# Two chained transformer blocks on one core: scaling the first block's attention queries whole, and moving its modulation sums to the end of a head

## The chip, the cores and the metric

One NeuronCore of a Trainium2 chip runs the whole program in one launch. The metric is the device time of that launch in microseconds (us), as the median of several runs. PE is TensorE (matrix products), DVE is VectorE, ACT is ScalarE, POOL is GpSimd and SP is SyncE, which here only issues transfers.

## The reference, cut to what matters

A first block (modulated normalisation, two kinds of attention, a gated feed-forward with a convolution) is followed by two layers of a second block. Everything is float32, 512 positions of 1024 features. The change lies in the first block's attention of eight heads, each with 64 unrotated and 32 rotated features:

```
mod = silu(c) @ w_ada + b_ada                # 6 * 1024 modulation values
sh1, sc1, g1, sh2, sc2, g2 = split(mod, 6)
h = rms_norm(x, g_mix_norm) * (1 + sc1) + sh1
q_lat, kv_lat, k_pe, qd, kd, vd = split(h @ w_in, SPLITS)
q = (rms_norm(q_lat, g) @ w_q_b).reshape(B, S, 8, 64 + 32)
q_nope, q_pe = rms_norm(q[..., :64], g), rope(rms_norm(q[..., 64:], g), positions)
kv = (rms_norm(kv_lat, g) @ w_kv_b).reshape(B, S, 8, 64 + 64)
k_nope, v = rms_norm(kv[..., :64], g), kv[..., 64:]
k_pe = rope(rms_norm(k_pe, g), positions)    # one rotated key part, shared by the 8 heads
o_mla = attention(cat(q_nope, q_pe), cat(k_nope, k_pe), v)
o_dil = dilated_attention(rope(norm(qd)), rope(norm(kd)), vd)
x = x + g1 * (cat(o_mla, o_dil) @ w_o)       # and then the feed-forward
```

## The kernel before

Each engine has a program of its own, written out by hand, and runs it strictly in that order. Semaphores tie the programs together: `at("head", t)` is the moment at which step `head` of tile `t` is done, and `wait_ge(*at(...))` waits for it.

**Weights** come as units of 1 MB, in the fixed order `STREAM`, through two buffers, `raw0` and `raw1`, in turn. SP issues unit v only when unit v-2, which lay in the same buffer, has been used. ACT copies a unit to a rounded high part (`split`, tile `whi`), DVE makes the low part (`wlo`), and PE does three products for each block (high x high, high x low, low x high; `mm3`).

Between the weight units lie units of `w_ada` for the modulation values. These aren't split. DVE's `ada_acc(a)` multiplies the eight parts of unit a by silu(c) and adds them up: two instructions on `128x256`, six more, and one that adds two halves. The raw buffer is free after the last of the six. PE's `ada_sums(a)` adds over the partitions, and DVE's `ada_out(a)` reads that sum into `mod`. The stream around the first block's heads is

```
a11, z8, a12, a13, z10, a14, a15, z12, a16, a17, z14, a18, a19, z16, wo0, wo1
```

where z8 to z16 are the units of the projections for the dilated attention and wo0 the first of `w_o`. So z10 comes into the buffer that a12 frees, z12 into that of a14, z14 into that of a16, z16 into that of a18, and wo0 into that of a19.

**Scaling.** After the projections, DVE works out the reciprocal roots r of all the norms. PE's `scale(t, b)` spreads the row of r that belongs to tile t over the partitions in PSUM bank b, and DVE's `head(t, b)` multiplies tile t by it: `qn` (unrotated query parts, 4 tiles of two heads), `qp` (rotated query parts, 2 tiles of four heads at 32 partitions each), `kn` (unrotated key parts), and `values_ok` for the values `vt`. The results of `qn` and `qp` go to `qt`, of `kn` to `kt`, where a head has 96 partitions. POOL sends the shared rotated key part to `kt` by a transfer once the last `qp` is scaled.

**The loop over heads.** In head h, PE does half of a projection tile (`z_half(h+2, 0)`), transposes two of the three parts of the probabilities (`head_turn(h, (0, 1))`), does the other half, transposes the last part (`head_turn(h, (2,))`), and then does the scores of head h+1, a row of statistics, the products with the values (`head_mix`), and `ada_sums(11 + h)`. ACT does, in this order, the split of the next z unit if h is odd (`split(9 + h // 2)`), the copies out of the transposes (`head_turned(h)`), the copies of the projection tile (`z_out`), and the exponentials of head h+1. The last part of `head_turn` waits for the first copy of `head_turned`. DVE finds the row maxima of head h+1 (`head_top`), multiplies a rotated tile by sines (`sine`) and does the sums `ada_acc`. POOL does the rest of the rotation (`rotate`) on `z` tiles.

Of the kernel before, what the change touches and what calls it, by code (L numbers as in the profile page):

```python
# [13 lines left out]
P = 128  # L14
S = 512
# [45 lines left out]
UNITS = split_units()  # L61
# [132 lines left out]
def build(nc, wstream, ada_in, x_in, pos_in, cols_in, layer_in, const_in, strip_in, bucket_in, rel_in, lru_in, y_out):  # L194
    scratch = nc.dram_tensor("bias_by_distance", (8, 640), F32, kind="Internal").ap()
    strips_dram = nc.dram_tensor("bias_strips", (8, P, S), F32, kind="Internal").ap()
    with ExitStack() as ctx:
# [51 lines left out]
        qn, qp, kn = region("qn", 17, [P, 4, S]), region("qp", 21, [P, 2, S]), region("kn", 4, [P, 4, S])  # L249
        qt, kt_ = region("qt", 9, [P, 8, S]), region("kt", 17, [P, 8, S])  # L250
        mla_out = [(region(f"mla_hi{i}", 9 + 2 * i, [P, S], F32R), region(f"mla_lo{i}", 10 + 2 * i, [P, S], F32R)) for i in range(4)]
        vt, zv = region("vt", 25, [P, 4, S]), region("zv", 17, [P, 4, S])
# [156 lines left out]
        def pe_program(pe):  # L409
# [231 lines left out]
            def head_scores(h, *free):  # L641
                for step in free:
                    pe.wait_ge(*at(*step))
                pe.wait_ge(*at("head", ("kn", h // 2)))
                pe.wait_ge(*at("k_pe"))
                if h > 0:
# [19 lines left out]

            def head_values(h):

                pe.wait_ge(*(at("values_ok", h // 2) if h < 8 else at("tile", ("z", 8 + (h - 8) // 2))))
                if h:  # L670
                    pe.wait_ge(*at("turned", h - 1, 1))
                src = vt[:, h // 2, :] if h < 8 else zv[:, (h - 8) // 2, :]
                for j in range(4):
                    ins = pe.transpose(ps[:, 4, P * j:P * (j + 1)], src[:, P * j:P * (j + 1)], C("ident"))
                ins.then_inc(*inc("values", "values", h))

            def head_turn(h, banks):
                maps = E[h % 2] if h < 8 else E_pair[h // 2][h % 2]
                pe.wait_ge(*(at("exp", h) if h < 8 else at("norm", h)))
                for b in banks:  # L680
                    if b == 2:
                        pe.wait_ge(*at("turned", h, 0))
                    elif b == 1 and h % 2 == 0:
                        pe.wait_ge(*at("vtok", h))
                    else:
                        pe.wait_ge(*(at("turned", h - 1, 2 - b) if h else at("head", ("kn", 2))))
                    for j in range(4):
# [57 lines left out]
            for n, t in enumerate(PROJECTED):  # L745
# [13 lines left out]
                if t == ("v", 2):  # L759
                    scale(("qn", 1), 0, ("head", "pe"))  # L760
                    scale(("qn", 2), 1, ("head", ("qn", 0)))
            z_half(0, 0, 6, ("sin", ("qp", 1)))
            scale(("qn", 3), 0, ("head", ("qn", 1)))
            scale(("qp", 0), 1, ("head", ("qn", 2)))
            z_half(0, 1, 6)
            scale(("qp", 1), 0, ("head", ("qn", 3)))
            statistics(("z", 0))
            scale("rms", 1, ("head", ("qp", 0)))
            scale(("kn", 0), 3)
            z_half(1, 0, 6, ("moved", ("z", 0)))  # L770
            scale(("kn", 1), 5, ("tile", ("v", 2)))
            z_half(1, 1, 6)
            scale(("kn", 2), 3, ("head", ("kn", 0)))
            scale(("kn", 3), 5, ("head", ("kn", 1)))
            head_scores(0, ("values_ok", 3), ("head", ("qp", 1)))
            statistics(("z", 1))
            head_values(0)
            for h in range(8):
                z_half(h + 2, 0, 6, ("moved", ("z", h + 1)) if h < 7 else ("tile", ("z", 8)))
                if h % 2 == 0 and h:  # L780
# [9 lines left out]
                if h < 7:  # L790
                    head_scores(h + 1)
                if h == 0:
                    head_turn(h, (2,))
                if h < 6:
# [5 lines left out]
                head_mix(h, *([("head", ("kn", 3))] if h == 0 else []))  # L800
                ada_sums(11 + h, 3, 0)
# [328 lines left out]
        def act_program(act):  # L1130
# [212 lines left out]
            for t in PROJECTED:  # L1343
# [8 lines left out]
                if t == ("kn", 1):  # L1352
                    split(7)
            head_seed("kv", 2, 10, KV_EPS)
            z_out(0, 6)
            split(8)
            z_out(1, 6)

# [41 lines left out]
            for h in range(8):  # L1400
                if h % 2 == 0 and h:
                    pair_out(h // 2 - 1)
                if h % 2:
                    split(9 + h // 2)
                if h == 0:
                    z_out(h + 2, 6)
                head_turned(h)
                if h:
                    z_out(h + 2, 6)
                if h == 5:  # L1410
# [240 lines left out]
        def dve_program(dve):  # L1651
# [284 lines left out]
            def head(t, b):  # L1936
# [10 lines left out]
                elif t[0] == "qp":  # L1947
                    dve.wait_ge(*at("roped", t))
                    for i in range(4):
                        w = slice(32 * i, 32 * i + 32)  # L1950
                        ins = dve.tensor_tensor(qt[64:96, 4 * t[1] + i, :], tile[w], ps[w, b, :], ALU.mult)
                else:
                    dve.wait_ge(*at("roped", t))
                    ins = dve.tensor_tensor(tile, tile, bank(b, rows), ALU.mult)
# [24 lines left out]
            head(("qn", 2), 1)  # L1979
            head(("qn", 3), 0)  # L1980
            head(("qp", 0), 1)
            head(("qp", 1), 0)
            sine(("z", 0))
            dve.wait_ge(*at("scale", "rms"))
            for i in range(4):
                dve.wait_ge(*at("tile", ("v", i)))
                dve.tensor_tensor(vt[:, i, :], vt[:, i, :], bank(1), ALU.mult).then_inc(*inc("values_ok", "values_ok", i))
            head(("kn", 0), 3)
            split(8)
            head(("kn", 1), 5)  # L1990
            head(("kn", 2), 3)
            head(("kn", 3), 5)


            def head_top(h):
                dve.wait_ge(*at("scores", h))
                if h == 0:
                    dve.wait_ge(*at("strip", 0))
                if h >= 2:
                    dve.wait_ge(*at("turn", h - 2, 2))  # L2000
# [62 lines left out]

            head_top(0)
            sine(("z", 1))
            ada_acc(11)
            for h in range(8):
                if h:
                    ada_out(10 + h, 3, 0)
                if h % 2 == 0 and h:  # L2070
                    pair_out(h // 2 - 1)
                if h == 6:
                    head_root("z", 7, 16, EPS[0:16])
                ada_acc(12 + h)
                if h % 2:
# [8 lines left out]
                if h % 2:  # L2084
                    pair_otok(h // 2)
            ada_out(18, 3, 0)
            pair_top(4, 0)
            pair_out(3)
            head(("z", 1), 7)
# [465 lines left out]
        def sp_program(sp):  # L2555
# [20 lines left out]
            for v in range(1, len(STREAM)):  # L2576
                load(v)
            for j, n in ((0, 2), (2, 2), (4, 2), (6, 1), (7, 1)):
                sp.wait_ge(*at("y", j + n - 1))
# [188 lines left out]
```

## Time and profile before

| | |
|---|---|
| Median of 3 runs | 2580.55 us (2578.91 to 2582.14) |
| Profiled execution, its own time | 2578.19 us |
| Its span | 2576.9 us |
| PE busy | 2530.8 us, 98% of the span |
| DVE, ACT, POOL busy | 1243.1, 953.3, 173.8 us |
| PE busy from 100 to 150 us | 40.85 of 50 us |
| PE busy from 500 to 1000 us | 500.00 of 500 us |

The span goes from the first to the last instruction. The first block's heads lie from about 150 to 253 us. In the rows below, a row of the timeline gives start, duration, engine, line, operation, output and inputs, and the count of merged instructions. A bracket at its end is the idle time of that engine just before it, and who ended it.

### The profile page before, as it was taken

To read this page: it belongs to the slowest core of one execution; us is meant where nothing else is said; L and a number is where in the kernel's file an instruction comes from. 1 tells how busy PE (TensorE), PEld (TensorE's weight loads), DVE (VectorE), ACT (ScalarE), POOL (GpSimd) and SP (SyncE) were. 2 spreads that over 40 slices of the span, in tenths; PEclk is the share of its full clock that TensorE was granted. 3 is DMA by queue.
4 is the path that set the end of the run, shared out by engine and by line. 5 is a ranking of instruction groups with operands and counts; after the bars stand their busy time and mean duration, and the time that the engine had idled before them with its cause. 6 is when DMAs were issued, how large, how long until landed. Compare 5 with 4: busy or idle time off the path is not lost.

```text
span 2576.9 us, 27632 instructions
## 1 busy us (share of the span) xinstructions
PE 2530.8 (98%) x11505; PEld 2052.2 (80%) x11505; DVE 1243.1 (48%) x1773; ACT 953.3 (37%) x1296; POOL 173.8 (7%) x172
## 2 busy tenths in 40 slices
PE   8989999999999999999999999999999999999998
PEld 5668778888888888878788888888888777888886
DVE  6677666654343333355743333433333466533333
ACT  5456544443232222335532222322222355422221
POOL 1121000000001110000011100011100000011100
PEclk9999999999999999999999999999999999999999
DMA  7333123333322222322232223222222322222231
GB/s 291 140 107 135 50 81 106 126 113 100 113 98 98 98 98 98 121 93 66 82 102 96 97 98 115 98 98 98 99 98 98 123 73 83 93 93 94 96 115 65
DMA packets 41390, 267.20 MB, mean 104 GB/s; under 512 B 5449, under 2 KB 5833, under 8 KB 11698
## 3 DMA queue, kind: packets, MB, share of 16 engines
q1 hardware_dynamic: 37440, 256.92, 29.1%
q0 software_dynamic: 2576, 7.10, 0.8%
q8 instruction: 91, 1.49, 0.2%
q10 hardware_dynamic: 1250, 1.42, 0.2%
q14 instruction: 33, 0.27, 0.0%
HBM read 262.78 MB, written 4.21 MB: 104 GB/s over the span
## 4 chain that ended last, share of the span: by engine, by line
PE 95%; DVE 3%; issue 1%; ACT 1%; DMA 0%; SPq 0%; DVEq 0%; ACTq 0%
PE ps L412 29%; PE ps L414 29%; PE ps L413 29%; PE ps L965 1%; PE ps L691 1%; PE ps L708 1%; PE ps L650 1%; PE ps L999 1%; DVE wlo L1655 0%; PE ps L580 0%; PE ps L664 0%; PE ps L986 0%; DMA early<-ada_in 0%; PE ps L582 0%; PE ps L581 0%
## 5 line engine op out<-in xcount | busy, mean ns | idle before, releaser
L1655 DVE TENSOR_TENSOR wlo<-raw,whi 128x2048 fp32r<-128x2048 f32 x213 | 488.1, 2292 | 1066.6 <-ACT whi L1137 1066.5
L412 PE MATMUL ps<-ahi,whi 128*128 128x512 f32 x2272 | 895.9, 394 | 1.3 <-ACT tmp L1321 1.3
L414 PE MATMUL ps<-alo,whi 128*128 128x512 f32 x2272 | 885.5, 390 | 0.0
L413 PE MATMUL ps<-ahi,wlo 128*128 128x512 f32 x2272 | 884.8, 389 | 0.0
L1137 ACT ACTIVATE whi<-raw 128x2048 fp32r<-128x2048 f32 x213 | 407.8, 1914 | 884.9 <-PE ps L414 882.6
L412 PEld LDWEIGHTS ps<-ahi,whi 128*128 128x128 f32 x2272 | 427.1, 188 | 94.8 <-issue 7.4
L414 PEld LDWEIGHTS ps<-alo,whi 128*128 128x128 f32 x2272 | 426.7, 188 | 90.0
L413 PEld LDWEIGHTS ps<-ahi,wlo 128*128 128x128 f32 x2272 | 427.1, 188 | 88.9 <-issue 2.6
L412 PE MATMUL ps<-hhi,whi 128*128 128x512 f32 x1008 | 393.1, 390 | 3.3 <-DVE hhi L2295 3.3
L413 PE MATMUL ps<-hhi,wlo 128*128 128x512 f32 x1008 | 392.2, 389 | 0.0
L414 PE MATMUL ps<-hlo,whi 128*128 128x512 f32 x880 | 342.3, 389 | 0.0
L412 PEld LDWEIGHTS ps<-hhi,whi 128*128 128x128 f32 x1008 | 189.2, 188 | 44.5 <-DVE hhi L2295 4.7
L413 PEld LDWEIGHTS ps<-hhi,wlo 128*128 128x128 f32 x1008 | 189.2, 188 | 39.0
L2522 POOL TENSOR_TENSOR tmp<-tmp,rstd 128x512 f32<-128x512 f32 x88 | 111.7, 1290 | 1550.2 <-ACT tmp L1477 1550.2
L414 PEld LDWEIGHTS ps<-hlo,whi 128*128 128x128 f32 x880 | 165.2, 188 | 34.4
L1484 ACT ACTIVATE hhi<-tmp 128x512 fp32r<-128x512 f32 x110 | 68.0, 636 | 176.8 <-DVE tmp L2191 130.1
L1477 ACT ACTIVATE tmp<-tmp 128x512 f32<-128x512 f32 x110 | 68.1, 632 | 165.2 <-DVE tmp L2186 133.2
L2197 DVE TENSOR_TENSOR hlo<-tmp,hhi 128x512 fp32r<-128x512 f32 x110 | 71.3, 690 | 5.3
L2155 DVE SCALAR_TENSOR_TENSOR tmp<-ps,cols,tmp 128x511 f32<-128x511 f32 (+1 forms) x88 | 59.7, 741 | 0.0
L2186 DVE TENSOR_TENSOR tmp<-ps,rstd 128x512 f32<-128x512 f32 x88 | 56.4, 682 | 0.0
L2191 DVE TENSOR_TENSOR tmp<-tmp,ps 128x512 f32<-128x512 f32 x88 | 56.2, 681 | 0.0
L2223 DVE TENSOR_TENSOR z<-ps,rstd 128x512 f32<-128x512 f32 x44 | 29.9, 687 | 49.5 <-PE ps L414 49.2
(389 smaller groups left out, 1717.0 us busy)
## 6 DMA issues: line engine op xcount, KB each, us to landing
raw<-wstream SPq DMA_DIRECT2D x221, 1024.0 KB, 4.8
raw<-wstream SPq DMA_DIRECT2D x24, 512.0 KB, 5.1
early<-ada_in SPq DMA_DIRECT2D x8, 1024.0 KB, 20.5
strip<-bias_strips POOLq DMA_DIRECT2D x16, 256.0 KB, 3.9
x<-x_in SPq DMA_DIRECT2D x2, 1024.0 KB, 6.6
bias_strips<-bias_by_distance POOLq DMA_DIRECT2D x1, 2048.0 KB, 16.6
y_out<-x SPq DMA_DIRECT2D x3, 512.0 KB, 2.7
bd<-lru_in ACTq DMA_DIRECT2D x2, 256.0 KB, 3.4
```

What stands on the lines that cost most here:

```text
L412: pe.matmul(out, wh, rhi, start=start, stop=False)
L413: pe.matmul(out, wl, rhi, start=False, stop=False)
L414: return pe.matmul(out, wh, rlo, start=False, stop=stop)
L1137: act.activation(hi_of(u)[:], raw[AT[UNITS[u]] % 2][:], ACT.Copy).then_inc(*inc("hi", "hi", u))
L1477: act.activation(tmp[m][:], tmp[m][:], ACT.Silu).then_inc(*inc("silu", "silu", f, i, m))
L1484: act.activation(hhi[:, 2 * i + m, :], tmp[m][:], ACT.Copy).then_inc(*inc("h_hi", "h_hi", f, 2 * i + m))
L1655: dve.tensor_tensor(lo_of(u)[:], raw[r][:], hi_of(u)[:].bitcast(F32), ALU.subtract).then_inc(*inc("lo_dve", "lo", u))
L2155: dve.scalar_tensor_tensor(tmp[b][:, d:], bank(b, n=S - d), col(w, j), tmp[b][:, d:], ALU.mult, ALU.add)\
L2186: dve.tensor_tensor(tmp[m][:], bank(m), rstd[:], ALU.mult).then_inc(*inc("gate_out", "gate_out", f, i, m))
L2191: dve.tensor_tensor(tmp[m][:], tmp[m][:], bank(2 + m), ALU.mult)\
L2197: dve.tensor_tensor(hlo[:, 2 * i + m, :], tmp[m][:], hhi[:, 2 * i + m, :].bitcast(F32), ALU.subtract)\
L2522: pool.tensor_tensor(tmp[m][:], tmp[m][:], rstd[:], ALU.mult).then_inc(*inc("silu_r", "silu_r", f, i, m))
```

## The change

It has three parts.

1. **The rotated query parts.** One DVE instruction over all 128 partitions scales a `qp` tile into a new tile `q_turned`, where four instructions of 32 partitions wrote it to `qt`. SP then sends the four heads' parts to `qt` by four transfers per tile, each issued after the tile's scaling (they stand in SP's program between the loads of z8 and a12). The scores wait for these transfers.
2. **More banks for the factors.** `scale` now uses banks 3, 5, 4 and 0 too, so that PE writes the factors of `qn` 3 and both `qp` tiles at once. The projection tile z1 goes to bank 7, and so the statistics of z0 and z1 come after both are read. Head 0's scores need only `kn` 0 and values tile 0; the other values and `kn` 1 to 3 are scaled afterwards. ACT splits z8 before it copies out z0, and copies head 0's transposes before projection tile 2.
3. **The modulation sums.** On DVE, `ada_out(11 + h)` and `ada_acc(12 + h)` now stand at the end of head h. Before, `ada_out(10 + h)` and `ada_acc(12 + h)` stood at its beginning. `ada_acc(19)` moves behind the loop, after the first row maxima of the dilated attention. `STREAM` is as it was.

```diff
@@ PE, scaling
+            scale(("qn", 3), 3, ("r", "q"))
+            scale(("qp", 0), 5, ("tile", ("v", 2)))
+            scale(("qp", 1), 4, ("tile", ("v", 3)))
             z_half(0, 0, 6, ("sin", ("qp", 1)))
-            scale(("qn", 3), 0, ("head", ("qn", 1)))
-            scale(("qp", 0), 1, ("head", ("qn", 2)))
             z_half(0, 1, 6)
-            scale(("qp", 1), 0, ("head", ("qn", 3)))
-            statistics(("z", 0))
-            scale("rms", 1, ("head", ("qp", 0)))
-            scale(("kn", 0), 3)
-            z_half(1, 0, 6, ("moved", ("z", 0)))
-            scale(("kn", 1), 5, ("tile", ("v", 2)))
-            z_half(1, 1, 6)
-            scale(("kn", 2), 3, ("head", ("kn", 0)))
-            scale(("kn", 3), 5, ("head", ("kn", 1)))
-            head_scores(0, ("values_ok", 3), ("head", ("qp", 1)))
-            statistics(("z", 1))
-            head_values(0)
+            scale(("kn", 0), 0, ("head", ("qn", 1)))
+            z_half(1, 0, 7, ("sin", ("qp", 0)))
+            scale("rms", 3, ("head", ("qn", 3)))
+            scale(("kn", 1), 5, ("head", ("qp", 0)))
+            z_half(1, 1, 7)
+            head_scores(0, ("head", ("qn", 2)), ("r", "kv"))
+            head_values(0, ("head", ("qp", 1)))
             for h in range(8):
...
+                if h == 0:
+                    pe.wait_ge(*at("moved", ("z", 1)))
+                    statistics(("z", 0))
+                    statistics(("z", 1))
+                    scale(("kn", 2), 0, ("top", 0))
+                    scale(("kn", 3), 1)
@@ ACT
             head_seed("kv", 2, 10, KV_EPS)
+            split(8)
             z_out(0, 6)
-            split(8)
-            z_out(1, 6)
+            z_out(1, 7)
...
-                if h == 0:
-                    z_out(h + 2, 6)
                 head_turned(h)
-                if h:
-                    z_out(h + 2, 6)
+                z_out(h + 2, 6)
@@ DVE, in head()
                 elif t[0] == "qp":
                     dve.wait_ge(*at("roped", t))
-                    for i in range(4):
-                        w = slice(32 * i, 32 * i + 32)
-                        ins = dve.tensor_tensor(qt[64:96, 4 * t[1] + i, :], tile[w], ps[w, b, :], ALU.mult)
+                    ins = dve.tensor_tensor(q_turned[:, t[1], :], tile, bank(b), ALU.mult)
@@ DVE, before the loop over heads
-            for i in range(4):
-                dve.wait_ge(*at("tile", ("v", i)))
-                dve.tensor_tensor(vt[:, i, :], vt[:, i, :], bank(1), ALU.mult).then_inc(*inc("values_ok", "values_ok", i))
-            head(("kn", 0), 3)
+            values_ok(0)
             split(8)
-            head(("kn", 1), 5)
-            head(("kn", 2), 3)
-            head(("kn", 3), 5)
...
             head_top(0)
+            for i in range(1, 4):
+                values_ok(i)
+            head(("kn", 1), 5)
+            head(("kn", 2), 0)
+            head(("kn", 3), 1)
             sine(("z", 1))
             ada_acc(11)
             for h in range(8):
-                if h:
-                    ada_out(10 + h, 3, 0)
                 if h % 2 == 0 and h:
                     pair_out(h // 2 - 1)
                 if h == 6:
                     head_root("z", 7, 16, EPS[0:16])
-                ada_acc(12 + h)
                 if h % 2:
                     split(9 + h // 2)
                 head_sum(h)
...
                 if h % 2:
                     pair_otok(h // 2)
-            ada_out(18, 3, 0)
+                ada_out(11 + h, 3, 0)
+                if h < 7:
+                    ada_acc(12 + h)
             pair_top(4, 0)
+            ada_acc(19)
             pair_out(3)
@@ SP
             for v in range(1, len(STREAM)):
                 load(v)
+                if STREAM[v] == UNITS[8]:
+                    for n in range(2):
+                        sp.wait_ge(*at("head", ("qp", n)))
+                        for i in range(4):
+                            sp.dma_start(qt[64:96, 4 * n + i, :], q_turned[32 * i:32 * i + 32, n, :])\
+                                .then_inc(*land(f"d_qpe{n}", *(("q_pe", n) if i == 3 else ("q_pe_part", n, i))))
```

The first place is DVE around the scaling. Before, its order from the last `qn` tiles to the last `kn` tiles was:

```order
L1946 SCALAR_TENSOR_TENSOR qt<-qn,gains,ps 64x512 x4
L1951 TENSOR_TENSOR qt<-qp,ps 32x512 x8
L1915 TENSOR_TENSOR tmp_77<-tmp_77,sin_dil 128x512
L1987 TENSOR_TENSOR vt<-vt,ps 128x512 x4
L1946 SCALAR_TENSOR_TENSOR kt<-kn,gains,ps 64x512 x2
L1655 TENSOR_TENSOR wlo_53<-raw_49,whi_51 128x2048
```

Now it is, up to the first row maximum of head 0:

```order
L1952 SCALAR_TENSOR_TENSOR qt<-qn,gains,ps 64x512 x4
L1955 TENSOR_TENSOR q_turned<-qp,ps 128x512 x2
L1952 SCALAR_TENSOR_TENSOR kt<-kn,gains,ps 64x512 x2
L1992 TENSOR_TENSOR vt<-vt,ps 128x512
L1921 TENSOR_TENSOR tmp_77<-tmp_77,sin_dil 128x512
L1661 TENSOR_TENSOR wlo_53<-raw_49,whi_51 128x2048
L2012 ISA E_127,stat_81<-ps,strip_row 128x512
```

Eight instructions on `qp` became two, and three on `vt` and six on `kn` moved behind head 0's maxima.

The second place is DVE from the sum of a12 (in `raw_50`, which is `raw1`) to the low part of z10, which uses the same buffer after it. Before:

```order
L1743 SCALAR_TENSOR_TENSOR tmp_78<-raw_50,small,tmp_78 128x256 x6
L1745 TENSOR_TENSOR tmp_78<-tmp_78 128x256
L2049 RECIPROCAL sel<-stat_81 128x4
L2005 ISA E_127,stat_82<-ps,strip_row 128x512
...
L1915 TENSOR_TENSOR tmp_77<-tmp_77,sin_dil 128x512
L1749 TENSOR_TENSOR mod<-ps,cols 128x2
L1740 TENSOR_SCALAR tmp_79<-raw_49,small 128x256 x2
L1743 SCALAR_TENSOR_TENSOR tmp_79<-raw_49,small,tmp_79 128x256 x6
L1745 TENSOR_TENSOR tmp_79<-tmp_79 128x256
L1655 TENSOR_TENSOR wlo_54<-raw_50,whi_52 128x2048
```

Now:

```order
L1755 TENSOR_TENSOR mod<-ps,cols 128x2
L1746 TENSOR_SCALAR tmp_78<-raw_50,small 128x256 x2
L1749 SCALAR_TENSOR_TENSOR tmp_78<-raw_50,small,tmp_78 128x256 x6
L1751 TENSOR_TENSOR tmp_78<-tmp_78 128x256
L1661 TENSOR_TENSOR wlo_54<-raw_50,whi_52 128x2048
```

The row maxima, the sines and the sum of a13 no longer lie between the last read of a12 and the split of z10 in the same buffer. The same is so at heads 3, 5 and 7. The third place is SP, which now issues eight small transfers between the loads of z8 and a12:

```order
L2581 DMA raw_50<-wstream 128x2048
L2581 DMA raw_49<-wstream 128x2048
L2594 DMA qt<-q_turned 32x512 x8
L2581 DMA raw_50<-wstream 128x2048
L2581 DMA raw_49<-wstream 128x2048
```

Before, the loads stood there without a gap. A wait for the scaling of `qp` now stands ahead of the load of a12.

## Rows read from the trace of the kernel before

**Rows 1.** The page, busy time by engine.

```profile
PE 2530.8 (98%) x11505; PEld 2052.2 (80%) x11505; DVE 1243.1 (48%) x1773; ACT 953.3 (37%) x1296; POOL 173.8 (7%) x172
```

**Rows 2.** Timeline of PE: its waits from 124 to 250 us, and two starts.

```profile
123.88 0.39 PE L412 MATMUL ps<-ahi,whi 128*128 128x512 f32 x1
...
130.40 0.80 PE L631 MATMUL ps<-r_q,rows 128*128 128x512 f32 x1 [3.41 <-DVE qt L1946]
...
136.26 1.13 PE L603 MATMUL ps<-sq,sel 128*128 128x512 f32 x2 [0.95 <-ACT sq L1296]
...
139.13 0.47 PE L412 MATMUL ps<-ahi,whi 128*128 128x512 f32 x1 [1.29 <-ACT tmp L1321]
...
147.55 0.51 PE L634 MATMUL ps<-r_kv,rows 128*128 128x512 f32 x1 [2.19 <-DVE kt L1946]
...
161.66 0.41 PE L691 MATMUL ps<-const,E 128*128 128x128 f32 x2 [1.63 <-ACT PT L1384]
...
165.39 0.48 PE L412 MATMUL ps<-ahi,whi 128*128 128x512 f32 x1
...
169.82 1.06 PE L691 MATMUL ps<-const,E 128*128 128x128 f32 x8 [1.42 <-issue]
...
173.47 0.38 PE L691 MATMUL ps<-const,E 128*128 128x128 f32 x2
...
246.46 1.06 PE L691 MATMUL ps<-const,E 128*128 128x128 f32 x8 [0.75 <-issue]
```

**Rows 3.** Windows: length, busy times, granted clock (1.00 is full), DMA share, GB/s.

```profile
130.00:132.00 2.00, 1.60 (x4) 1.32 (x5) 1.92 (x4) 0.00 (x0) 0.00 (x0) 0.53 0.00 0
132.00:134.00 2.00, 2.00 (x7) 1.54 (x6) 1.96 (x4) 0.00 (x0) 0.00 (x0) 0.62 0.00 0
```

**Rows 4.** Timeline of DVE: the scaling (`qp`, `vt`, `kn`).

```profile
135.35 2.78 DVE L1951 TENSOR_TENSOR qt<-qp,ps 32x512 f32<-32x512 f32 x4 [0.66 <-PE ps L631]
...
139.74 2.48 DVE L1987 TENSOR_TENSOR vt<-vt,ps 128x512 f32<-128x512 f32 x4
...
145.99 4.58 DVE L1946 SCALAR_TENSOR_TENSOR kt<-kn,gains,ps 64x512 f32<-64x512 f32 x6
```

**Rows 5.** The key part's transfer: timeline of POOL, and the line's landing time.

```profile
138.43 0.67 POOL L2503 DMA_DIRECT2D kt<-kpe  x1 [26.82 <-DVE qt L1951]
...
DMA to landing us min/median/max: 4.7/4.7/4.7
```

**Rows 6.** SP's loads from 180 to 250 us, and the page's half units.

```profile
L2569 SPq DMA_DIRECT2D raw<-wstream x7: 328/328/328, 187.4 to 241.7; - x7
DMA to landing us min/median/max: 4.7/4.9/5.0
...
raw<-wstream SPq DMA_DIRECT2D x24, 512.0 KB, 5.1
```

**Rows 7.** Timeline of DVE: a modulation sum at the start of head 3.

```profile
193.09 1.66 DVE L1740 TENSOR_SCALAR tmp<-raw,small 128x256 f32<-128x256 f32 x2 [0.32 <-issue]
194.67 2.46 DVE L1743 SCALAR_TENSOR_TENSOR tmp<-raw,small,tmp 128x256 f32<-128x256 f32 x6
```

**Rows 8.** Timeline of POOL at the same time.

```profile
193.16 1.43 POOL L2485 TENSOR_TENSOR zk<-zk,tmp 128x512 f32<-128x512 f32 x1
```

**Rows 9.** Timeline of DVE: the sum of a12, POOL being idle.

```profile
161.84 0.81 DVE L1740 TENSOR_SCALAR tmp<-raw,small 128x256 f32<-128x256 f32 x2 [4.29 <-DMA raw<-wstream]
162.57 2.45 DVE L1743 SCALAR_TENSOR_TENSOR tmp<-raw,small,tmp 128x256 f32<-128x256 f32 x6
```

**Rows 10.** Head 3: ACT's split of z12, and PE's last transposes.

```profile
193.38 1.90 ACT L1137 ACTIVATE whi<-raw 128x2048 fp32r<-128x2048 f32 x1
...
198.90 0.38 PE L691 MATMUL ps<-const,E 128*128 128x128 f32 x2
```

**Rows 11.** Behind the heads: DVE's first dilated maxima done, PE's next tile (z11).

```profile
259.26 0.27 DVE L2029 TENSOR_SCALAR stat<-stat 128x2 f32<-128x2 f32 x2
...
261.46 0.48 PE L412 MATMUL ps<-ahi,whi 128*128 128x512 f32 x1
```

More of the change, by code:

```diff
@@ L250, in build @@
         qt, kt_ = region("qt", 9, [P, 8, S]), region("kt", 17, [P, 8, S])
+        q_turned = region("q_turned", 35.5, [P, 2, S])
         mla_out = [(region(f"mla_hi{i}", 9 + 2 * i, [P, S], F32R), region(f"mla_lo{i}", 10 + 2 * i, [P, S], F32R)) for i in range(4)]
@@ L645, in head_scores @@
                 pe.wait_ge(*at("k_pe"))
+                if h % 4 == 0:
+                    pe.wait_ge(*at("q_pe", h // 4))
                 if h > 0:
@@ L665, in pair_scores, with head_values @@
                 ins.then_inc(*inc("scores", "pair_scores", p, step))
-            def head_values(h):
+            def head_values(h, *free):
+                for step in free:
+                    pe.wait_ge(*at(*step))
                 pe.wait_ge(*(at("values_ok", h // 2) if h < 8 else at("tile", ("z", 8 + (h - 8) // 2))))
@@ L685, in head_turn @@
                     else:
-                        pe.wait_ge(*(at("turned", h - 1, 2 - b) if h else at("head", ("kn", 2))))
+                        pe.wait_ge(*(at("turned", h - 1, 2 - b) if h else at("values_ok", 3)))
                     for j in range(4):
@@ L761, in pe_program @@
                     scale(("qn", 2), 1, ("head", ("qn", 0)))
+            scale(("qn", 3), 3, ("r", "q"))
+            scale(("qp", 0), 5, ("tile", ("v", 2)))
+            scale(("qp", 1), 4, ("tile", ("v", 3)))
             z_half(0, 0, 6, ("sin", ("qp", 1)))
-            scale(("qn", 3), 0, ("head", ("qn", 1)))
-            scale(("qp", 0), 1, ("head", ("qn", 2)))
             z_half(0, 1, 6)
-            scale(("qp", 1), 0, ("head", ("qn", 3)))
-            statistics(("z", 0))
-            scale("rms", 1, ("head", ("qp", 0)))
-            scale(("kn", 0), 3)
-            z_half(1, 0, 6, ("moved", ("z", 0)))
-            scale(("kn", 1), 5, ("tile", ("v", 2)))
-            z_half(1, 1, 6)
-            scale(("kn", 2), 3, ("head", ("kn", 0)))
-            scale(("kn", 3), 5, ("head", ("kn", 1)))
-            head_scores(0, ("values_ok", 3), ("head", ("qp", 1)))
-            statistics(("z", 1))
-            head_values(0)
-            for h in range(8):
-                z_half(h + 2, 0, 6, ("moved", ("z", h + 1)) if h < 7 else ("tile", ("z", 8)))
+            scale(("kn", 0), 0, ("head", ("qn", 1)))
[5 more added lines that the diff above has]
+            head_values(0, ("head", ("qp", 1)))
+            for h in range(8):
+                z_half(h + 2, 0, 6, ("moved", ("z", h + 1 if h else 0)) if h < 7 else ("tile", ("z", 8)))
+                if h == 0:
[4 more added lines that the diff above has]
+                    scale(("kn", 3), 1)
                 if h % 2 == 0 and h:
@@ L790, in pe_program @@
                 if h < 7:
-                    head_scores(h + 1)
+                    head_scores(h + 1, *([("head", ("kn", 2)), ("head", ("kn", 3))] if h == 0 else []))
                 if h == 0:
                     head_turn(h, (2,))
+                    head_mix(h, ("head", ("kn", 1)))
                 if h < 6:
@@ L799, in pe_program @@
                     scale(("z", 4), 7, ("head", ("z", 0)))
-                head_mix(h, *([("head", ("kn", 3))] if h == 0 else []))
+                if h:
+                    head_mix(h)
                 ada_sums(11 + h, 3, 0)
@@ L1979, in dve_program, with values_ok @@
             head(("qn", 2), 1)
-            head(("qn", 3), 0)
-            head(("qp", 0), 1)
-            head(("qp", 1), 0)
-            sine(("z", 0))
-            dve.wait_ge(*at("scale", "rms"))
-            for i in range(4):
-                dve.wait_ge(*at("tile", ("v", i)))
-                dve.tensor_tensor(vt[:, i, :], vt[:, i, :], bank(1), ALU.mult).then_inc(*inc("values_ok", "values_ok", i))
-            head(("kn", 0), 3)
+            head(("qn", 3), 3)
+            head(("qp", 0), 5)
+            head(("qp", 1), 4)
+            head(("kn", 0), 0)
+            def values_ok(i):
+                dve.wait_ge(*at("scale", "rms"))
+                dve.wait_ge(*at("tile", ("v", i)))
+                dve.tensor_tensor(vt[:, i, :], vt[:, i, :], bank(3), ALU.mult).then_inc(*inc("values_ok", "values_ok", i))
+            values_ok(0)
+            sine(("z", 0))
             split(8)
-            head(("kn", 1), 5)
-            head(("kn", 2), 3)
-            head(("kn", 3), 5)
             def head_top(h):
@@ L1998, in head_top @@
                     dve.wait_ge(*at("strip", 0))
+                if h == 1:
+                    dve.wait_ge(*at("q_pe", 0))
+                    dve.wait_ge(*at("q_pe", 1))
                 if h >= 2:
```

## Prediction

> **What bounds the kernel now.** I began with the page. PE is busy for 2530.8 us of 2576.9 [rows 1], so a change can only give back PE's waits, or add to them. Next I listed the waits on PE's timeline. Between 124 us and head 1's start at 165.39 there are five: 3.41, 0.95, 1.29, 2.19 and 1.63, together 9.47 us. After it there are 1.42 at 169.82 and 0.75 at 246.46 [rows 2]. Otherwise PE runs through the heads without a gap. The first four waits are for DVE's scaling or ACT's copies. Then I looked at the clock: in the 4 us after the wait of 3.41 the granted clock was 0.53 and 0.62 (the lower level, 1.2 GHz, for most of it) [rows 3]. Lost there: 1.60 x 0.47 + 2.00 x 0.38 = 1.5 us. So the region that the change touches holds at most 9.5 + 1.5 + 1.4 + 0.75 = 13.1 us.
>
> **The front (parts 1 and 2).** The factors of `qn` 3 and both `qp` no longer wait for a bank, so the waits at 130.40 and 136.26 go. Scaling two `qp` tiles costs DVE two instructions at 2.48 / 4 = 0.62 us in place of twice 2.78 [rows 4], and three `vt` (1.9) and six `kn` (4.6) instructions move behind head 0's maxima. `qp` 1 was done at 135.35 + 2.78 = 138.1. Now DVE doesn't wait between the tiles and is done near 133.2. POOL's key transfer starts 0.3 us later and lands after 4.7 [rows 5]: 138.2. PE comes to head 0's scores at 123.88 + 0.7 (three factors) + 4 x 2.8 (half tiles) + 0.7 = 136.5. A half tile is (173.47 - 165.39 - 1.42 - 1.06) / 2 = 2.8 [rows 2]. So a new wait of 1.7 us stands there, for the key part.
>
> Eight sends from SP aren't in the trace. Their issue is 0.33 each [rows 6]. Their landing lies between nothing and the key part's 4.7 [rows 5]; at 4.7 the fourth lands at 132.6 + 3 x 0.33 + 4.7 = 138.3, beside the key part. I take that, so they cost 0.1. Queued behind them on SP is the load of a12, which waits until 153.9 for a11 in any case (below). A second new wait, before head 1, is for ACT: it now copies head 0's transposes before tile 2. I take 0.9, between 0 and the 1.29 of the same kind [rows 2].
>
> Front: +9.5 + 1.5 - 1.7 - 0.1 - 0.9 = 8.3 gained. Each wait also costs the overlap of one matmul (0.39 of duration against 0.23 of pitch), and there are three fewer: 8.7, I take 8.5. Head 1 starts at 156.9. The 1.42 at 169.82 came from DVE doing a12's sum ahead of head 1's maxima, and the 0.75 from a18's in the same way. Both sums now stand behind the maxima: 2.2 gained. **Gains: 10.7 us.**
>
> **The sums (part 3).** The work is the same, so its own cost is nothing. What moves is the moment at which a raw buffer is free. Before, a14 was read at the start of head 2, and z12, which follows in that buffer, had a whole head to arrive. Now a14 is read after `ada_out(13)`, that is after PE's end of head 2. ACT meets the split of z12 at the start of head 3, and queued behind it on ACT are the copies out of the transposes, for which PE waits. Nothing is left to cover the load.
>
> Head 3, on the clock of before. A sum that starts when PE has ended the head before is in the trace: two instructions at 193.09 and six to 194.67 + 2.46 = 197.1 [rows 7]. The load lands 4.9 later [rows 6], at 202.0. ACT's split takes 1.90 [rows 10] and its first copy 0.55: 204.5. PE wants the copy at 198.90 [rows 10]. **Wait: 5.6 us.** Head 5 is the same, 5.6. In head 7 POOL has no rotation left, and the first pair takes 0.81 in place of 1.66 [rows 7, 9]: 4.7.
>
> Head 1. The request for a12 was at 161.84 - 4.7 = 157.1. Head 0's scores start at 138.3, not 147.9 (9.6 earlier), but 1.9 + 4.6 of `vt` and `kn` now come between: 157.1 - 9.6 + 6.5 = 154.0. a12 lands at 158.7, its parts take 3.2 [rows 9], z10 lands at 166.8, split and copy end at 169.2. PE is there at 156.9 + 2.8 + 0.9 + 2.8 = 163.4. **Wait: 5.8.**
>
> Behind the heads. a19's sum comes after maxima that end at 259.53 [rows 11]. Add 3.2 for the parts, 5.1 for the load in two halves [rows 6], 1.9 for ACT's split, 0.6 for its copy of z10's tile: 270.3. PE wants that bank at 261.46 [rows 11]. **Wait: 8.9.**
>
> The five are 5.8 + 5.6 + 5.6 + 4.7 + 8.9 = 30.6 us. All are longer than the 3.41 that was followed by the low clock, so each gets its 1.5 us: 7.5. A single such place in the trace bears this, so the bounds are 0 and 5 x 2 = 10 (the 4 us of [rows 3] all at 1.2 GHz).
>
> The Trainium skill ("TensorE: Matmul & The Clock Gate", What's actually happening) says that the throttled clock is the default and activity releases it. By that rule all five waits cost clock, and the sum is the one with 7.5; were the row a chance event, it would be 7.5 less.
>
> The pair of instructions took 1.66 while POOL's addition ran at 193.16 and 0.81 while it was idle [rows 7 to 9]. With the short pair everywhere, the waits of heads 3 and 5 would be 0.85 less each, 1.7 together. I take the long one, since the sum again follows `sine`, for which POOL's addition waits.
>
> The Trainium skill ("SBUF — State Buffer", Who interferes with whom) gives a rule of this kind: VectorE in a two-port mode and GpSimd take a shared port pair in turn, and the later one blocks. By it the long pair stays in heads 3 and 5; without it the forecast would be 1.7 less.
>
> **Sum.** 30.6 + 7.5 - 10.7 = +27.4 on the profiled execution's 2578.19: 2605.6. The median of the runs shown lies 2.4 above that execution, and single runs spread by 3. I forecast 2607.
>
> **The rivals.**
> *The reload is hidden* (faster). Only the gains are left: 2580.6 - 10.7 = 2570. For it: DVE and ACT are busy half the time, and a12's load of before was waited for by DVE alone. Against it: the chain from the sum to the first copy is 193.1 to 204.5, and PE reaches its end in 6. It decides once the five waits together fall under 10.7, about 2 each; that needs the load to land in under 2 us, where seven took 4.7 to 5.0 [rows 6]. Chance 0.06; no measurable change 0.04.
> *Waits without the clock*: full clock after them, or landings at the short end. 2580.6 + 30.6 - 10.7 = 2600, less 3.4 for short pairs and landings: 2597. Chance 0.17.
> *The small sends are late* (slower still). If four sends follow one another at 4.7 each [rows 5], the first scores start near 151.5 and not 138.3: 13 more, 2620. Against it: each holds 64 KB, and the key part with its 512 KB took 4.7 as a whole. Chance 0.08.
> *The waits as worked out*: 2600 to 2615, chance 0.65.
>
> **The numbers.** What a measurement here can tell from no change is about 0.2%, 5 us. Faster 0.06, same 0.04, slower 0.90. The range takes in the second rival and the late sends: 2592 to 2620. The likeliest case alone is 2600 to 2615.
>
> **What would show it.** In the trace after: head 1 starts near 157 us. PE waits for ACT's first copy of the transposes in heads 1, 3, 5 and 7, 4.5 to 6 us each; in front of it ACT waits for a load, and SP's load is issued right behind the sixth part of a sum. One wait near 9 us stands behind the heads. The granted clock falls after each. From 500 us on nothing changes but the offset. The forecast is wrong if ACT's splits of z10 to z16 start without waiting for a load, if the clock stays at full rate (7 too much), or if head 0's scores start later than 140 us.

## The result, and the profile after

The changed kernel takes 2620.1 us (median of 4 runs, 2618.1 to 2621.5), beside 2579.7 for the kernel before (4 runs, 2578.9 to 2582.1). The ratio is 1.0151, with a 95% interval of 1.0139 to 1.0164. It is slower, as forecast, but by 40.4 us and not by 27. 2620.1 lies at the very edge of the range of 2592 to 2620, and outside the 2600 to 2615 of the likeliest case.

The page of after. PE has 18.3 us more busy time for the same 11505 matmuls [rows 1], and its clock row falls to 8 tenths in three early slices of 65 us. Both say that matmuls ran slower, over and above the waits:

```profile
span 2619.6 us, 27641 instructions
PE 2549.1 (97%) x11505; PEld 2063.9 (79%) x11505; DVE 1238.9 (47%) x1767; ACT 953.5 (36%) x1296; POOL 174.3 (7%) x172
PEclk9988899999999999999999999999999999999999
```

The timeline of PE after, its long waits from 124 us on: start, duration, engine, line and operation, and in brackets the wait before it. These answer to [rows 2]:

```profile
140.33 4.61 PE L653 MATMUL ps<-kt,qt 96*128 96x512 f32 x8 [3.03 <-DMA qt<-q_turned]
161.58 0.47 PE L413 MATMUL ps<-ahi,whi 128*128 128x512 f32 x1 [0.82 <-ACT tmp L1330]
175.31 0.66 PE L696 MATMUL ps<-const,E 128*128 128x128 f32 x2 [7.16 <-ACT PT L1393]
209.04 0.66 PE L696 MATMUL ps<-const,E 128*128 128x128 f32 x2 [5.37 <-ACT PT L1393]
243.97 0.66 PE L696 MATMUL ps<-const,E 128*128 128x128 f32 x2 [6.35 <-ACT PT L1393]
275.89 0.41 PE L696 MATMUL ps<-const,E 128*128 128x128 f32 x2 [4.37 <-ACT PT L1393]
301.74 0.77 PE L413 MATMUL ps<-ahi,whi 128*128 128x512 f32 x1 [9.46 <-ACT zv L1333]
```

The five waits of the front are gone; so are the 1.42 and the 0.75. In their place stand one wait of 3.03 in the front, one of 0.82 for ACT's tile 2, and the five that the prediction named: 7.16 + 5.37 + 6.35 + 4.37 + 9.46 = 32.7 us. All waits of PE from 124 us to 340 us are 38.2 us, and were 13.2: 24.9 more. The span is 42.7 longer, so some 18 us are not waits.

The windows of after, PE alone, over the 10 us (in head 7 the 14) behind each wait. The column behind PE's busy time is the granted clock. They answer to [rows 3]:

```profile
140.33:150.33 10.00, 10.00 (x29) 0.68 0.07 16
175.31:185.31 10.00, 10.00 (x44) 0.72 0.01 2
209.04:219.04 10.00, 10.00 (x44) 0.70 0.00 1
243.97:253.97 10.00, 10.00 (x45) 0.74 0.00 0
275.89:289.89 14.00, 14.00 (x53) 0.63 0.00 1
301.74:311.74 10.00, 10.00 (x35) 0.73 0.36 107
```

The time lost to the clock is the length of a window times what its clock lacks of 1.00: 3.2 in the front, then 2.8, 3.0, 2.6, 5.2 and 2.7. The five big waits lose 16.3 us in this way, all six 19.5; before had 1.5. That is 18.0 more, which with the 24.9 of waits makes 42.9. Another 0.9 was there before the change begins: the first matmul on the factors starts at 121.11 us in this execution and at 120.24 before. That makes 43.8, beside the 42.7 of the span.

One cycle of a head in full, head 1 after. ACT waits 8.88 us for the load of z10, splits it, and only then copies the transposes out:

```profile
172.64 1.91 ACT L1146 ACTIVATE whi<-raw 128x2048 fp32r<-128x2048 f32 x1 [8.88 <-DMA raw<-wstream]
174.57 1.09 ACT L1393 ACTIVATE PT<-ps 128x512 f32<-128x512 f32 x2
```

The load goes out behind the sixth part of DVE's sum of a12, which runs here (it answers to [rows 9]):

```profile
163.51 1.64 DVE L1746 TENSOR_SCALAR tmp<-raw,small 128x256 f32<-128x256 f32 x2 [1.28 <-DMA raw<-wstream]
165.07 2.45 DVE L1749 SCALAR_TENSOR_TENSOR tmp<-raw,small,tmp 128x256 f32<-128x256 f32 x6
```

The sum ends at 167.5, and ACT's split starts 5.1 later. Behind the heads nothing moved. The last 2279.6 us of both executions hold the same 10130 matmuls, with 2260.3 us of busy time before and 2260.4 after.

### The profile page after: what moved, and what is told of

It is laid out like the page before. It is cut to its first block, busy times and chain, and to the rows that moved or that the text cites. A ratio compares the mean times of both kernels' runs of the same rounds, so it can differ in the third digit from the quotient of the medians.

```text
span 2619.6 us, 27641 instructions
## 1 busy us (share of the span) xinstructions
PE 2549.1 (97%) x11505; PEld 2063.9 (79%) x11505; DVE 1238.9 (47%) x1767; ACT 953.5 (36%) x1296; POOL 174.3 (7%) x172
## 3 DMA queue, kind: packets, MB, share of 16 engines
q10 hardware_dynamic: 1250, 1.42, 0.2%
## 4 chain that ended last, share of the span: by engine, by line
PE 92%; DVE 4%; DMA 2%; issue 1%; ACT 1%; SPq 0%; DVEq 0%; ACTq 0%
PE ps L413 28%; PE ps L415 28%; PE ps L414 28%; DMA raw<-wstream 1%; PE ps L974 1%; PE ps L653 1%; DVE tmp L1749 1%; PE ps L713 1%; PE ps L696 1%; PE ps L1008 1%; PE ps L667 0%; DMA early<-ada_in 0%; PE ps L581 0%; PE ps L995 0%; PE ps L583 0%
```

## The experiments

The reading above names two causes, waits and clock, and one part of the change (the sums) for nearly all of both. The rivals are that the banks and sends of the front have a share, that the waits come from where ACT's split stands, and that the 18 us beyond the waits are something other than the clock. Eight kernels tell these apart. All were timed beside the kernel before, the first four on one chip (it took 2580.4 us there) and the last four on another (2580.7). So between kernels of the two groups the ratios to the kernel before are set beside the medians. Each diff below is against the changed kernel, or against the kernel that is named.

### The sums put back: parts 1 and 2 alone

```
             for h in range(8):
+                if h:
+                    ada_out(10 + h, 3, 0)
...
+                ada_acc(12 + h)
...
-                ada_out(11 + h, 3, 0)
-                if h < 7:
-                    ada_acc(12 + h)
+            ada_out(18, 3, 0)
...
-            ada_acc(19)
```

> The changed kernel with its modulation sums back at the start of a head (part 3 undone; parts 1 and 2 kept). Theory 'reload': the five long waits (7.2, 5.4, 6.4, 4.4 and 9.5 us, 32.7 in all) come from loads requested too late, and the low clock after them costs 14.8 us. Both go. But a12's sum now stands ahead of head 1's maxima again, while head 1 starts earlier than before against the landing of a12, so one wait of about 7 us (with 3 of clock) should stand ahead of head 1's first transposes, and 0.75 in head 7: about 2583 us. Rival 'front' (the sends and the new order of scaling are the loss): it stays above 2605.

Measured: 2580.5 us (2579.4 to 2583.3), ratio 1.0004 [0.9995, 1.0014]. The five waits are gone, and so are 39.6 us. But parts 1 and 2 bring nothing. PE's timeline of this kernel shows where their gain went:

```profile
139.78 3.43 PE L653 MATMUL ps<-kt,qt 96*128 96x512 f32 x8 [3.00 <-DMA qt<-q_turned]
...
159.56 0.47 PE L413 MATMUL ps<-ahi,whi 128*128 128x512 f32 x1 [0.82 <-ACT tmp L1330]
...
169.34 1.94 PE L696 MATMUL ps<-const,E 128*128 128x128 f32 x8 [6.79 <-issue]
```

Head 1 starts 5.8 us earlier than before (159.56 beside 165.39 [rows 2]), and 6.79 us are then waited for at its first transposes, where before waited 1.42. The releaser is not named, but DVE's timeline has it. DVE waits for the load of a12 and sums it ahead of head 1's maxima. The first row is the sum of a11, with which the load of a12 becomes possible:

```profile
154.26 2.46 DVE L1749 SCALAR_TENSOR_TENSOR tmp<-raw,small,tmp 128x256 f32<-128x256 f32 x6
...
161.41 0.61 DVE L1746 TENSOR_SCALAR tmp<-raw,small 128x256 f32<-128x256 f32 x2 [4.24 <-DMA raw<-wstream]
161.94 2.46 DVE L1749 SCALAR_TENSOR_TENSOR tmp<-raw,small,tmp 128x256 f32<-128x256 f32 x6
```

The sum of a11 ends at 156.7, where it ended at 157.1 before, since the scaling of `vt` and `kn` tiles now stands ahead of it. So the load of a12 goes out at the same time as before, for a head that starts 5.8 us earlier. The clock behind the two longer waits:

```profile
139.78:149.78 10.00, 10.00 (x34) 7.01 (x35) 5.84 (x15) 3.77 (x11) 1.29 (x2) 0.83 0.09 20
169.34:177.34 8.00, 8.00 (x26) 6.31 (x27) 4.86 (x9) 4.01 (x6) 0.00 (x0) 0.64 0.62 216
```

That is 1.7 and 2.9 us lost. (All engines are in the columns here; the clock is the third from the end.)

### The sums alone: part 3 put into the kernel before

The edit is the same, with the sign turned round, in the kernel before.

> The kernel before with part 3 alone (the sums at a head's end). 'Reload': waits of about 5.1, 5.4, 6.4, 4.4 and 9.5 us, 3 us of low clock after each, and the old waits of 1.42 and 0.75 gone: about +43 us, 2623 us, at least as slow as the whole change. 'Front': close to the kernel before, under 2595.

Measured: 2623.8 us (2619.4 to 2624.8), ratio 1.0166 [1.0150, 1.0181]. PE's waits in heads 1, 3, 5 and 7 are 4.32, 5.26, 6.32 and 3.86, and 9.73 stands behind the heads: 29.5 us together. So part 3 alone costs 43 us with the old front and 39.6 with the new one. It is the whole of the slowdown, within the spread of the runs.

### The waits filled with work

Five matmuls whose result nobody reads stand ahead of the last transposes of the odd heads, and nine ahead of z11, where PE would stand idle. Nothing that the kernel computes is left out.

```
+                for _ in range(5 if h % 2 else 0):
+                    pe.matmul(bank(0), C("ones"), x[:, 0, :], start=True, stop=True)
...
+            pe.wait_ge(*at("mod", 18))
+            for _ in range(9):
+                pe.matmul(bank(3), C("ones"), x[:, 0, :], start=True, stop=True)
```

> The changed kernel with 5 matmuls of 0.95 us (ones times x, 128x512, into a bank that is free) ahead of the last transposes of heads 1, 3, 5 and 7, and 9 ahead of tile z11. They add work that nothing reads, inside the waits. If idle time lowers the clock, most of the 14.8 us that the low clock costs behind these waits comes back: about 2606 us, and waits under 3 us remain at the same places. If the low clock has another cause, no change or slower: 2620 or more.

Measured: 2606.5 us (2605.0 to 2607.3), ratio 1.0101 [1.0086, 1.0116]. More work on PE makes the kernel 13.6 us faster. ACT's split of z10 starts at 172.59 here and at 172.64 without the filling, so the copies are ready no earlier, and this gain is no shorter wait; it is the clock. Windows of this kernel behind what is left of the waits (2.49, 1.11, 2.03 and 1.89 us; the fourth row is head 7, where no wait is left), with all engines in the columns ahead of the clock:

```profile
175.27:183.27 8.00, 8.00 (x48) 6.42 (x49) 6.60 (x17) 7.31 (x17) 3.08 (x2) 1.00 0.00 0
206.30:214.30 8.00, 8.00 (x47) 6.41 (x48) 6.54 (x19) 7.31 (x17) 0.00 (x0) 1.00 0.00 1
238.33:246.33 8.00, 8.00 (x41) 5.98 (x41) 4.81 (x14) 6.30 (x15) 2.51 (x2) 0.79 0.00 0
265.00:280.00 15.00, 15.00 (x72) 10.38 (x72) 7.00 (x18) 3.75 (x5) 0.00 (x0) 1.00 0.06 22
290.34:298.34 8.00, 7.65 (x35) 5.71 (x35) 5.81 (x16) 3.25 (x10) 0.00 (x0) 1.00 0.36 91
```

Only one of the five places still loses, 8 x 0.21 = 1.7 us. 16.3 - 1.7 = 14.6 us should come back by the windows, and 13.6 did.

### ACT's split moved behind the copies it held up

```
-                if h % 2:
-                    split(9 + h // 2)
...
+                if h % 2:
+                    split(9 + h // 2)
```

It now stands behind `head_turned` and `z_out`.

> The changed kernel with ACT's split of z10 to z16 behind the copies out of the transposes and the copies of the tile. If the copies wait only because they are queued behind the split on ACT, PE's waits at the last transposes of heads 1, 3, 5 and 7 go. The load is still late, so smaller waits should appear at the next use: for the low part of the unit and for the next head's exponentials, about 4.4 us in head 2 and 2 to 3 in the others; the wait of 9.5 behind the heads stays. 2597 to 2609 us. If the waits had nothing to do with ACT's order: 2620.

Measured: 2603.1 us (2601.6 to 2604.0), ratio 1.0088 [1.0072, 1.0105], 17.1 us better. The queue behind the split is confirmed as a part of the matter: PE no longer waits for the copies. It waits for the tile itself, in two hops, ACT's part and then DVE's `wlo`. PE's timeline:

```profile
175.57 0.50 PE L413 MATMUL ps<-ahi,whi 128*128 128x512 f32 x1 [2.40 <-DVE wlo L1661]
205.25 0.80 PE L413 MATMUL ps<-ahi,whi 128*128 128x512 f32 x1 [2.40 <-DVE wlo L1661]
...
235.73 0.80 PE L413 MATMUL ps<-ahi,whi 128*128 128x512 f32 x1 [2.40 <-DVE wlo L1661]
262.93 0.80 PE L413 MATMUL ps<-ahi,whi 128*128 128x512 f32 x1 [2.95 <-DVE wlo L1661]
283.55 0.77 PE L413 MATMUL ps<-ahi,whi 128*128 128x512 f32 x1 [9.57 <-ACT zv L1333]
```

The four are 10.2 us in place of 23.3. The load itself is late, wherever ACT stands. The last, behind the heads, does not depend on this split and is all but unchanged at 9.57 (9.46). Two details of the expectation failed: the wait of head 2 is 2.40 and not 4.4, and PE has none for the exponentials. The clock behind the four:

```profile
175.57:183.57 8.00, 8.00 (x34) 6.62 (x35) 7.67 (x24) 4.48 (x12) 1.28 (x1) 0.79 0.12 16
205.25:213.25 8.00, 8.00 (x31) 6.54 (x32) 7.19 (x24) 4.47 (x12) 0.00 (x0) 0.68 0.13 17
235.73:243.73 8.00, 8.00 (x30) 6.50 (x31) 7.93 (x24) 5.60 (x14) 1.28 (x1) 0.66 0.07 10
262.93:270.93 8.00, 8.00 (x23) 5.44 (x24) 2.25 (x9) 0.00 (x0) 0.00 (x0) 0.66 0.00 0
```

They lose 1.7, 2.6, 2.7 and 2.7, together 9.7, where the four places lost 13.6 in the changed kernel. So 13.1 us less of waits and 3.9 less of clock make up the 17.1.

### The banks without the sends

Against the first experiment: `qp` is scaled in four pieces straight into `qt`, and the eight sends are left out.

```
-                    ins = dve.tensor_tensor(q_turned[:, t[1], :], tile, bank(b), ALU.mult)
+                    for i in range(4):
+                        w = slice(32 * i, 32 * i + 32)
+                        ins = dve.tensor_tensor(qt[64:96, 4 * t[1] + i, :], tile[w], ps[w, b, :], ALU.mult)
```

> The sums are where they were before, the banks are the changed kernel's, and the rotated query parts are scaled in four pieces straight into their place, with no sends. The row of before gives 2.78 us for four such pieces, two tiles of them 5.6 us, where the whole tiles took 2.6. DVE then gives the rotated key part to POOL some 3 us later, it lands near 143.7 us, and head 0's scores start about 4 us later than with the sends; the wait there is 6 to 7 us in place of 3.0. If the sends and whole scaling are worth their cost: 2584 (2582 to 2587), against 2580.5 with them. If the banks did the work and the sends only cost their issue of 0.59 us each and their landing: 2579 or less.

Measured: 2584.3 us (2582.5 to 2585.8), ratio 1.0014 [1.0004, 1.0023]; 3.8 above the first experiment, or 2.6 by the two ratios. DVE's scaling takes 5.59 us in place of 1.28, and the wait ahead of head 0's scores is 4.85 after one of 1.27. The scaling of whole tiles and the sends are worth some 3 us together, so the sends' cost is smaller than what they save.

### The queries ahead of the key root

Against the first experiment: DVE scales `qn` 2 and 3 and both `qp` before it computes the reciprocal roots of the keys, and PE does one half tile before it makes the key factors.

```
-            head_root("kv", 2, 10, KV_EPS)
...
+            head_root("kv", 2, 10, KV_EPS)
```

> The sums are where they were before; DVE scales the last query tiles ahead of the key root, so the eight sends start earlier. If the wait of 3.0 us at head 0's scores is for the sends and the key part behind qp on DVE, it goes, with the 2.9 us of half clock that follow it, and DVE's later work (the key tiles) gives back a little: 2574.5 (2573 to 2577). If the wait only moves, to the key root or the key tiles (PE waits as long at the key scaling): 2580 to 2581, as without it.

Measured: 2576.3 us (2574.7 to 2577.2), ratio 0.9982 [0.9973, 0.9991]; 4.2 better than the first experiment, or 5.7 by the two ratios, as by the two spans. The wait of 3.0 is gone, and head 0's scores are followed by a clock of 1.00. (In the first experiment that wait was followed by a loss of 1.7 us, not of the 2.9 that the expectation has.) The wait in head 1 stays, and grows from 6.79 to 7.30. The gain isn't lost there this time, since the sum of a11 also ends 5.7 us earlier, and with it the load of a12 goes out at 151.1 and not at 156.7. The first send goes out at 128.3 and not at 133.0, right behind DVE's scaling: the sends are late because DVE gives `q_turned` late, and not because of SP.

### The sum of a11 ahead of head 0's maxima

Against the first experiment:

```
             split(8)
+            ada_acc(11)
...
             sine(("z", 1))
             for h in range(8):
...
-            ada_acc(11)
```

> The sums are where they were before, except the one on a11, which now stands ahead of head 0's maxima, where DVE was idle 5.8 us waiting for the scores. Theory: the wait of 6.8 us at head 1's first transposes is for DVE, which did a12's sum ahead of head 1's maxima and had waited 4.2 us for a12's load; with a11's sum early, a12 lands before DVE wants it and the wait goes, with the clock after it: 2573 (2571 to 2576). Rival: head 0's maxima come later for the sum ahead of them (3 to 4 us of it not covered), PE waits at head 0's transposes instead: 2577 to 2581.

Measured: 2572.2 us (2570.8 to 2572.5), ratio 0.9965 [0.9953, 0.9978]. It is the fastest of all and beats both kernels, the one before by 0.35% and the changed one by 48 us. It keeps parts 1 and 2, leaves the sums of a12 to a19 as they were before, and does that of a11 where DVE was idle, for 5.8 us in the changed kernel and for 4.6 in the first experiment. PE's timeline has one wait above 1.1 us from 124 to 340 us, the one for the sends:

```profile
138.48 4.60 PE L653 MATMUL ps<-kt,qt 96*128 96x512 f32 x8 [3.09 <-DMA qt<-q_turned]
159.62 0.47 PE L413 MATMUL ps<-ahi,whi 128*128 128x512 f32 x1 [0.82 <-ACT tmp L1330]
```

The wait of 6.79 at head 1's first transposes is gone. In the first experiment it lost 2.9 us of clock on top (0.64 over 8 us). Both together are 9.7 us; the spans of the two profiled executions differ by 9.6 (2579.1 and 2569.5), the medians by 8.3. That the two agree so well is in part chance: at the `qn` tiles this execution was already 1.4 us ahead, and the wait for the sends cost it 1.4 us more of clock (0.69 over 10 us, beside 0.83).

### Both edits

> Both edits: query tiles ahead of the key root, and a11's sum ahead of head 0's maxima. If the two waits are independent, the gains add, less a wait of about 2.9 us at head 1's scores for the scaling of key tiles 2 and 3, which now stands behind the sum: 2570 (2568 to 2573). If DVE becomes the bound of the first block, it gives no more than the better of the two alone: 2573 to 2576.

Measured: 2572.7 us (2570.5 to 2574.3), ratio 0.9969 [0.9957, 0.9980]: the same as the better of the two alone. The time by itself doesn't decide: it lies in the range of the first theory and 0.3 us under that of the second. The trace speaks for the second. PE's waits are no shorter in sum than with a11's sum alone (5.0 and 4.7 us from 124 to 250 us); DVE's work behind head 0's scores stands end to end, and PE waits for it in other places:

```profile
146.67 1.22 PE L635 MATMUL ps<-r_kv,rows 128*128 128x512 f32 x2 [2.12 <-DVE stat L2017]
153.00 2.40 PE L653 MATMUL ps<-kt,qt 96*128 96x512 f32 x8 [0.41 <-DVE kt L1952]
```

From 143 to 153 us DVE is busy for 9.79 of 10 us there.

## Why the prediction was right in the sign and short in the size

**The mechanism held.** The forecast said that the sum at a head's end leaves nothing to cover the load, and that ACT's split queues the copies behind it. The trace after shows it link by link, the sums alone cost 43 us in the kernel before, and taking them back gives 39.6. Where the split was moved, the wait for the copies went, and 10.2 of the 23.3 us came back at the tile itself.

**The five waits** were forecast as 30.6 and are 32.7. By place: head 1 7.16 for 5.8, head 3 5.37 for 5.6, head 5 6.35 for 5.6, head 7 4.37 for 4.7, behind the heads 9.46 for 8.9. Of these the first is worst. That the front was late didn't lengthen it: a12's load landed 4.8 us later than forecast (163.5 for 158.7), but PE too came to its last transposes 4.7 later (168.15 for 163.4). What did is DVE's pair, 1.64 us with POOL's addition beside it, for which the forecast took the short 0.81; the load of z10 (5.1 for 4.9), the split and the copy give the rest. In head 5 the same work took DVE 1.57 and 3.49, where the forecast had 1.66 and 2.46.

**The term that failed is the clock**, "each gets its 1.5 us: 7.5", with 10 as its upper bound. That the stated range still reaches the measured time is luck: its upper end stood there for the sends being late, which didn't happen. Measured: 16.3 for the same five waits, between 2.6 and 5.2 each. The 1.5 was read from one place of before, where half rate lasted 3 to 4 us, and was carried to waits up to three times as long. I bounded the term by the 4 us of those rows; behind a wait of 4 to 9 us, half rate lasted 5 to 10. The step was 8.8 us too small. It is shown to be the clock by the filled waits: with the same ready times, and more work, 13.6 us came back.

The single place was also a poor one to measure by. The sums alone have the same instructions and the same wait of 3.41 there, and run on at full clock. Windows of that kernel, all engines:

```profile
131.00:135.00 4.00, 2.58 (x11) 2.16 (x12) 3.89 (x6) 0.00 (x0) 0.00 (x0) 1.00 0.00 0
```

**The front** was forecast as 8.5 gained. Its waits were 3.03 and 0.82 for a sum of 2.7, which is 1.2 more. The rest is the clock again: the 1.5 of before was taken as gained, and no loss was put down to the new waits. The one of 3.03 cost 3.2 (one of 3.00 cost 1.7 in the first experiment). So 8.5 - 1.2 - 3.2 = 4.1 is left; head 1 starts at 161.58 where 156.9 was forecast. By the forecast's own sign, scores of head 0 later than 140 us, the front was wrong: they started at 140.33. Of the two transfers, the key part went out at 134.4 and landed in 5.5 us and not in 4.7 [rows 5], at 139.9. SP's issues took 0.59 us each and not 0.33, but for the fourth (1.83) and the fifth (1.55), and the eight landed in 2.0 to 4.8. The fourth, the last that head 0's scores need, was issued at 135.4 and took 4.8: it landed at 140.2, and the scores started at 140.33. In the row, 133.5 and 140.1 are the starts of the first and the last issue:

```profile
L2594 SPq DMA_DIRECT2D qt<-q_turned x8: 587/592/1832, 133.5 to 140.1; - x8
...
DMA to landing us min/median/max: 2.0/2.6/4.8
```

**The other gains.** The 1.42 and 0.75 went, as forecast (2.2). In sum: 27.4 + 0.9 (start) + 1.2 (front's waits) + 3.2 (front's clock) + 2.1 (the five waits) + 8.8 (their clock) = 43.6, beside a span 42.7 longer; 0.9 stays unexplained.

**Without part 3** the forecast would have been wrong in another way: "the reload is hidden" counts 10.7 gained, 2570. The first experiment has no reload in the way and gave 2580.5. The gain of the front is lost there at head 1's first transposes. I had taken that wait as 1.42 for any start of head 1, while it depends on when a12 lands, and so on when DVE has summed a11. In the changed kernel the error is out of sight, since the sum stands behind the maxima. With a11's sum early the 2570 was nearly reached (2572.2), by an edit that the forecast didn't have.

**The small sends late**, at 2620 with 0.08, gave the measured number by a wrong path: the scores start at 140.33 and not at 151.5.

**The clock rule.** The Trainium skill ("TensorE: Matmul & The Clock Gate", What's actually happening) has the low rate as the default, which activity lifts. By it all five waits would cost clock, and all five did, so the trace of after agrees. The price, near 3 us a wait, is from the windows above alone.

**The short pair.** It came in head 3 after, as 0.71 us, but the six parts behind it then took 3.48 in place of 2.45 [rows 9]; in head 1 it was 1.64 and 2.45. In head 5 both were long. Beside POOL's work DVE lost 0.8 us in head 1, 1.0 in head 3 and 1.8 in head 5, so taking the long pair was nearly right for head 3, too little for head 5, and it was missing in head 1.

## What to carry to other kernels

Before work that frees a buffer is moved later, look for the next user of that buffer and for what is queued behind this user on its engine: here eight sums that moved by about a head cost 40 us together, since the loads came late and ACT's split of the reloaded tile stood ahead of copies that PE wanted. On a kernel whose PE is otherwise full, price an idle stretch of several us as the stretch plus the half rate behind it, and take the latter from more than one place. And a gain in front of a load that does not move with it is lost at that load: moving one sum into idle time of DVE was worth 8 us or more after the front had been worth nothing.

## What the runs showed of the hardware

- After waits of 4.4 to 9.5 us PE ran at half rate (1.2 GHz) for 5 to 10 us more, at 100% busy. The longest stretch, in head 7, followed the shortest of these waits (4.37): the clock was 0.63 over 14 us. So the length of a wait does not set the price. In head 7 the clock stood at 1.00 through the whole wait and for the first 0.5 us of work after it, and was low only from 276.4 to 286.6 us; behind the heads it was low (0.50) in the last 3.7 us of the wait already, so that a part of the low stretch fell on idle time.
- Short waits are uneven. Three of 2.40 us were followed by 0.79, 0.68 and 0.66 over 8 us, one of 2.49 and one of 1.11 by 1.00, and one of 2.03 by 0.79. A wait of 3.03 cost 3.2 us and one of 3.00 at the same place 1.7. The same wait of 3.41 cost 1.5 us in one kernel and nothing in another. What decides it stays open; no run here tells it.
- Matmuls that nobody needs, put into a wait, saved 13.6 us.
- POOL's and DVE's instructions on SBUF delay one another. The timeline of POOL in the kernel with the early sum:

```profile
135.16 3.24 POOL L2497 TENSOR_TENSOR zq<-zq,tmp 128x512 f32<-128x512 f32 x1 [0.67 <-DVE tmp L1921]
139.37 1.37 POOL L2494 TENSOR_TENSOR zq<-zq,cos_dq 128x512 f32<-128x512 f32 x1 [0.96 <-ACT tmp L1330]
152.94 1.31 POOL L2497 TENSOR_TENSOR zq<-zq,tmp 128x512 f32<-128x512 f32 x1 [12.20 <-DVE tmp L1921]
```

and that of DVE, beside it:

```profile
135.00 2.29 DVE L1661 TENSOR_TENSOR wlo<-raw,whi 128x2048 fp32r<-128x2048 f32 x1
137.20 1.62 DVE L1746 TENSOR_SCALAR tmp<-raw,small 128x256 f32<-128x256 f32 x2
138.74 3.46 DVE L1749 SCALAR_TENSOR_TENSOR tmp<-raw,small,tmp 128x256 f32<-128x256 f32 x6
```

The same addition takes 1.31 alone and 3.24 when it starts 0.16 us behind DVE's `wlo`, which ends at 137.3; the addition ends 1.1 us later, and DVE's pair, begun in between, takes 1.62. DVE's six parts take 3.46 with POOL's product beside them and 2.45 alone [rows 9]. The Trainium skill ("SBUF — State Buffer", Who interferes with whom) states such a turn-taking for an instruction of VectorE with two inputs in SBUF, as `wlo` has, and these rows agree. It cost PE nothing here: DVE was still 0.46 us early for head 0's maxima.
